# Decays relative to a tile's edge or the half's end: the reference column as the bias of ScalarE's exponential, tile by tile, instead of a subtraction on VectorE

## The chip, the cores and the metric

One core of one Trainium2 chip. The metric is the device time of one execution in microseconds (us); the profile is that of one execution, read on the same core.

## The reference

The program runs two transformer-like blocks over 256 tokens of width 2048. The part at issue is the RWKV-7 recurrence of the second block, 16 heads of 64:

```python
log_w = -jax.nn.softplus(-(w0 + jnp.tanh(pw) @ w2)) - 0.5
decay = jnp.exp(-jnp.exp(log_w))
...
def step(state, xs_t):
    r_t, w_t, k_t, v_t, kk_t, a_t = xs_t
    sa = jnp.einsum('bhvk,bhk->bhv', state, -kk_t)
    state = (state * w_t[:, :, None, :] + sa[..., None] * (kk_t * a_t)[:, :, None, :]
             + v_t[..., None] * k_t[:, :, None, :])
    return state, jnp.einsum('bhvk,bhk->bhv', state, r_t)
```

With s = sigmoid(w0 + ...), the logarithm of the decay is -exp(-0.5) s. The product of decays between two positions is therefore exp(-DECAY x (difference of two running sums of s)), with DECAY = exp(-0.5).

## The kernel before

The heads are taken in two halves of 8 (`hf` = 0, 1), one after the other, and the tokens in two tiles of 128, so the recurrence becomes matrix products inside a tile plus a state between the two tiles. In each half the operands lie as [128 partitions, J = 4, T = 256]: 1024 columns, j the pair of heads, two token tiles of 128 in each j. `CUM` is the running sum of s within each tile, `LDX` the same without the token's own share. R, K, KKN and AA are the receptance, the key, the normalised key and KKN times the gate a.

Each operand is multiplied by a decay relative to some reference point, so that the exponentials stay in range. There are four kinds of reference: the middle of each block of 64 tokens (`mid`, for KRD and BKD), the last token of the first half of each tile (`edge`, for KRO and BKO, which serve the block below the diagonal), the end of the first tile (`end`, for BKS, which carries the state), and the tile's start (nothing to subtract, for KRS).

VectorE (`rw_dve`, from L2079) forms the differences: `arg` (L2131) writes one into `EA[0]` or `EA[1]` and raises `decay_arg`. ScalarE (`rw_act`, from L1133) works through the list `tasks`: nine Exp instructions (L1166), each waiting for its `decay_arg` count and, through `decay_used`, until VectorE has done with the former contents of the buffer `EX[0]` or `EX[1]`. Behind the fourth and the fifth ScalarE also copies a tile of values out of PSUM (L1169). VectorE waits for Exp n with `expo(n)` and multiplies (`mul`, L2137). In order of VectorE's program between these: the bonus (L2157), the product BKO that raises `grams_ready`, an addition to the residual rows (`out_add`, L2087), BKS that raises `bks_ready`, and KRS that raises `decayed`.

The four differences for `edge` and `end` are of 512 columns, and so are the four Exps that read them. `EX[0]` and `EX[1]` are used several times, so the order of Exps and products is tied on both sides.

TensorE (`rw_pe`, from L2977) meanwhile multiplies pieces of the output projection (L2970). It then waits for `grams_ready`, takes the first pair of heads (L3036, L3044), waits for `bks_ready`, transposes BKS (L3029), which ScalarE copies out (L1172), and goes on with the other seven pairs, whose results VectorE masks (L2181). GpSimd clears a buffer after `decayed`. All engines run their own program in order; only semaphores tie them. No DMA is issued for this work.

Of the kernel before, what the change touches and what calls it, by code (L numbers as in the profile page):

```python
# [21 lines left out]
ALU = mybir.AluOpType  # L22
ACT = mybir.ActivationFunctionType
AX = mybir.AxisListType

P = 128
T = 256
# [18 lines left out]
DECAY = float(np.exp(-0.5))  # L46
# [85 lines left out]
def build(nc, a, out):  # L132
    ctx = ExitStack()
    with ctx:
# [47 lines left out]
        ev = Signals()  # L182
# [18 lines left out]
        def av(off, *dims):  # L201

            n = int(np.prod(dims))
            assert off + n <= 36984
            v = AR[:, off:off + n]
            if len(dims) == 2:
                v = v.rearrange("p (a b) -> p a b", a=dims[0])
            if len(dims) == 3:
                v = v.rearrange("p (a b c) -> p a b c", a=dims[0], b=dims[1])
            if len(dims) == 4:  # L210
                v = v.rearrange("p (a b c d) -> p a b c d", a=dims[0], b=dims[1], c=dims[2])
            return v
# [147 lines left out]
        J, HH = 4, 8  # L360
# [7 lines left out]
        EA = [YT[:, 12:16, :], av(21760, J, T)]  # L368
        EX = [av(33554, J, T), av(22784, J, T)]
# [8 lines left out]
        LDX = av(24576, J, T)  # L378
        AA = av(25600, J, T)
        CUM = av(34578, J, T)  # L380
# [4 lines left out]
        RY2 = av(35602, NT, 512)  # L385
        SAB = av(18432, 512)
        RST = av(36640, 4, 16)
        KSQ, RKP = av(0, J, T), av(5120, J, T)


# [20 lines left out]
        def part(x, n):  # L411

            return x[:, 2 * n:2 * n + 2, :].rearrange("p j (a s) -> p (j a) s", s=P)
# [3 lines left out]
        def flat(ap):  # L417
            n = len(ap.shape)
            if n == 3:
                return ap.rearrange("p a b -> p (a b)")  # L420
            if n == 4:
                return ap.rearrange("p a b c -> p (a b c)")
            return ap
# [709 lines left out]
        def rw_act(act, o, hf):  # L1133
            R, K, V = (RKVS[hf][:, w] for w in range(3))
            if hf == 1:
                act.wait_ge(ev["gn_out"], 2)
            for j in range(J):
                ins = nc.scalar.activation(KSQ[:, j, :], K[:, j, :], ACT.Square, scale=col2("kk", J * hf + j))
            o.tell(ins, ev["kk_sq"])
            for n, (dst, bias) in enumerate(((LDX, "w0"), (AA, "a0"), (GATE, None))):  # L1140
                act.wait_ge(ev["lora_mm"], 3 * hf + n + 1)
                for j in range(J):
                    b = 2 * (n % 2) + j // 2
                    src = PQ[:, b, (j % 2) * T:(j % 2 + 1) * T]
                    if bias:
                        ins = nc.scalar.activation(dst[:, j, :], src, ACT.Sigmoid, bias=col2(bias, J * hf + j))
                    else:
                        ins = nc.scalar.copy(dst[:, j, :], src)
                o.tell(ins, ev["lora_out"])
                if n == 1:  # L1150
                    act.wait_ge(ev["kk_mm"], hf + 1)
                    o.tell(nc.scalar.activation(KNORM[0:8, :], PP[0:8, 1, 0, 0:T], ACT.Sqrt), ev["kk_root"])
                    act.wait_ge(ev["lora_out"], 3 * hf + 2)
                    for j in range(J):
                        ins = nc.scalar.activation(EA[0][:, j, :], AA[:, j, :], ACT.Identity, scale=col2("ka", J * hf + j),
                                                   bias=OKA[:, J * hf + j:J * hf + j + 1])
                    o.tell(ins, ev["ka_out"])
            tasks = [(EX[0], EA[0], 1, 0, -1.0), (EX[1], EA[0], 1, 0, 1.0), (EX[0], EA[1], 2, 1, -1.0),
                     (part(EX[1], 0), part(EA[0], 0), 3, 2, -1.0), (part(EX[1], 1), part(EA[0], 1), 4, 2, -1.0),
                     (part(EX[0], 0), part(EA[1], 0), 5, 3, -1.0), (part(EX[0], 1), part(EA[1], 1), 6, 3, -1.0),  # L1160
                     (part(EX[1], 0), CUM[:, :, P:T], 6, 4, -1.0), (part(EX[1], 1), LDX[:, :, P:T], 6, 5, -1.0)]
            for n, (dst, src, args, uses, sign) in enumerate(tasks):
                act.wait_ge(ev["decay_arg"], 6 * hf + args)
                if uses:
                    act.wait_ge(ev["decay_used"], 5 * hf + uses)
                o.tell(nc.scalar.activation(dst, src, ACT.Exp, scale=sign * DECAY), ev["decay_exp"])  # L1166
                if n == 3 or n == 4:
                    act.wait_ge(ev["rv_turned"], 2 * hf + n - 2)
                    o.tell(nc.scalar.copy(VTK[:, n - 3, :], PQ[:, n - 3, :]), ev["rv_tok"])  # L1169
            for n in range(2):  # L1170
                act.wait_ge(ev["bk_turned"], 2 * hf + n + 1)
                o.tell(nc.scalar.copy(BKT[:, n, :], PQ[:, 2 + n, :]), ev["bk_tok"])  # L1172

            for m in range(16):
                act.wait_ge(ev["gram_diag"], 16 * hf + m + 1)
                o.tell(nc.scalar.copy(GR[0:64, m, :, 64:P], PP[0:64, (m % 4) // 2, m % 2, 0:256].rearrange("p (a t) -> p a t", a=4)),
                       ev["gram_out"])
            inverse_act(act, o, 1 + hf, GR[:, :, 0, :], RTI, RTT)
            for t in range(NT):
                n = 2 * hf + t + 1  # L1180
                act.wait_ge(ev["gn_mean"], n)
                o.tell(nc.scalar.activation(RY2[:, t, :], RY[:, t, :], ACT.Square), ev["gn_sq"])
                if t == 0:
                    nc.scalar.activation(SM[:, 8:9], EPSC, ACT.Sqrt)
                act.wait_ge(ev["gn_sum"], n)
                o.tell(nc.scalar.activation(RST[:, 1, 8 * t:8 * t + 8], RST[:, 0, 8 * t:8 * t + 8], ACT.Sqrt, scale=1.0 / 64,
                                            bias=RWEPSC), ev["gn_root"])
            if hf == 0:
                o.tell(nc.scalar.activation(RS, SS, ACT.Sqrt, scale=1.0 / D, bias=EPSC), ev["norm_root"])
# [889 lines left out]
        def rw_dve(dve, o, v, hf, diagonal):  # L2079
# [17 lines left out]
            for j in range(J):  # L2097
                for t in range(NT):
                    ins = v.tensor_tensor_scan(CUM[:, j, t * P:(t + 1) * P], ONES, LDX[:, j, t * P:(t + 1) * P], 0.0,
                                               ALU.mult, ALU.add)  # L2100
# [6 lines left out]
            for j in range(J):  # L2107
                ins = v.scalar_tensor_tensor(KKN[:, j, :], K[:, j, :], col2("kk", J * hf + j),
                                             PQ[:, 2 + j // 2, (j % 2) * T:(j % 2 + 1) * T], ALU.mult, ALU.mult)
# [3 lines left out]
            for j in range(J):  # L2113
                ins = v.scalar_tensor_tensor(RKP[:, j, :], R[:, j, :], col2("rk", J * hf + j), K[:, j, :], ALU.mult, ALU.mult)
# [2 lines left out]
            blocks = lambda x: x.rearrange("p j (b s) -> p (j b) s", s=64)  # L2117
            tiles = lambda x: x.rearrange("p j (t s) -> p (j t) s", s=P)
            mid = blocks(CUM)[:, :, 31:32].broadcast_to([P, 16, 64])
            edge = tiles(CUM)[:, :, 63:64].broadcast_to([P, 8, 64])  # L2120
            end = CUM[:, :, P - 1:P].broadcast_to([P, J, P])
            lo, hi = (lambda x: tiles(x)[:, :, 0:64]), (lambda x: tiles(x)[:, :, 64:P])

            half_of = lambda x, n: flat(x)[:, 512 * n:512 * (n + 1)]
            h = lambda x, n: half_of(x, n).rearrange("p (b s) -> p b s", s=64)
            w = lambda x, n: half_of(x, n).rearrange("p (j s) -> p j s", s=P)
            osl = lambda x: x.rearrange("p j t s -> p (j t) s")
            t0, t1 = (lambda x: x[:, :, 0:P]), (lambda x: x[:, :, P:T])

            def arg(out, x, y):  # L2130
                o.tell(v.tensor_tensor(out, x, y, ALU.subtract), ev["decay_arg"])  # L2131
# [4 lines left out]
            def mul(out, x, y):  # L2136
                return v.tensor_tensor(out, x, y, ALU.mult)  # L2137
# [3 lines left out]

            arg(blocks(EA[0]), blocks(CUM), mid)
            arg(blocks(EA[1]), blocks(LDX), mid)
            o.done(mul(AA, AA, KKN))
            expo(1)
            spent(mul(KRD[:, :, 1, :], R, EX[0]))
            expo(2)
            arg(h(EA[0], 0), hi(CUM), edge)
            arg(h(EA[0], 1), hi(LDX), edge)
            mul(BKD[:, 0], AA, EX[1])  # L2150
            spent(mul(BKD[:, 1], K, EX[1]))
            expo(3)
            arg(h(EA[1], 0), edge, lo(CUM))
            arg(w(EA[1], 1), end, t0(CUM))
            spent(mul(KRD[:, :, 0, :], KKN, EX[0]))
            dve.wait_ge(ev["bonus_mm"], hf + 1)
            o.tell(v.tensor_tensor(flat(BON), PQ[:, 2:4, :].rearrange("p a b -> p (a b)"), flat(V), ALU.mult), o.order)  # L2157
# [1 line left out]
            for j in range(J):  # L2159
                ins = mul(KRO[:, j, 1], h(EX[1], 0)[:, 2 * j:2 * j + 2, :], hi(R)[:, 2 * j:2 * j + 2, :])  # L2160
            spent(ins)
            expo(5)
            for j in range(J):
                ins = mul(KRO[:, j, 0], h(EX[1], 1)[:, 2 * j:2 * j + 2, :], hi(KKN)[:, 2 * j:2 * j + 2, :])
# [24 lines left out]
            n = 2 * hf  # L2189
# [53 lines left out]
            for j in range(J):  # L2243
                ins = v.scalar_tensor_tensor(BON[:, j, :], BON[:, j, :], col2("lnb", J * hf + j), GATE[:, j, :], ALU.add, ALU.mult)
# [1152 lines left out]
```

## Time and profile before

| | us |
|---|---|
| median of 3 runs | 3686.59 |
| lowest and highest | 3685.14, 3688.18 |
| the profiled execution | 3684.46 |
| its span in the profile | 3682.7 |

| engine | busy us | share of the span |
|---|---|---|
| TensorE (PE) | 3531.0 | 96% |
| TensorE weight loads (PEld) | 3084.2 | 84% |
| VectorE (DVE) | 2328.9 | 63% |
| ScalarE (ACT) | 1476.9 | 40% |
| GpSimd (POOL) | 77.2 | 2% |

The names in brackets are those of the profile's rows. Shares are over the whole span and hide that the stages differ; the stretch of the change is under 19 us long and comes twice. A matmul's end is modelled, and a few records can be missing. The idle time that a row shows is that of its engine just before it, with the instruction that ended it. Tiles of the large working buffer all have the name `arena`, columns of constants `constants`, PSUM banks `quad` and `pairs`.

### The profile page before, as it was taken

To read this page: it belongs to the slowest core of one execution; us is meant where nothing else is said; L and a number is where in the kernel's file an instruction comes from. 1 tells how busy PE (TensorE), PEld (TensorE's weight loads), DVE (VectorE), ACT (ScalarE), POOL (GpSimd) and SP (SyncE) were. 2 spreads that over 40 slices of the span, in tenths; PEclk is the share of its full clock that TensorE was granted. 3 is DMA by queue.
4 is the path that set the end of the run, shared out by engine and by line. 5 is a ranking of instruction groups with operands and counts; after the bars stand their busy time and mean duration, and the time that the engine had idled before them with its cause. 6 is when DMAs were issued, how large, how long until landed. Compare 5 with 4: busy or idle time off the path is not lost.

```text
span 3682.7 us, 51878 instructions
## 1 busy us (share of the span) xinstructions
PE 3531.0 (96%) x21246; PEld 3084.2 (84%) x21246; DVE 2328.9 (63%) x2679; ACT 1476.9 (40%) x1313; POOL 77.2 (2%) x110
## 2 busy tenths in 40 slices
PE   8997899999999999999999999988989989999998
PEld 8985799999988888888888799986657778888887
DVE  3655547977767776666666766466674556666666
ACT  4333433345543333333333433443332433333333
POOL 1000000000000000000000000000100000000000
PEclk9998999999999999999999999999999999999999
DMA  5552444556677675555555455431114445555553
GB/s 195 183 183 71 169 157 175 203 185 222 223 265 243 242 255 202 203 197 205 203 201 204 150 181 176 161 114 46 47 69 149 149 149 191 186 193 184 192 188 143
DMA packets 122755, 649.47 MB, mean 176 GB/s; under 512 B 10720, under 2 KB 43872, under 8 KB 49536
## 3 DMA queue, kind: packets, MB, share of 16 engines
q1 hardware_dynamic: 116368, 621.25, 47.7%
q0 software_dynamic: 6256, 26.34, 1.9%
q8 instruction: 98, 1.61, 0.2%
q14 instruction: 33, 0.27, 0.0%
HBM read 619.76 MB, written 27.79 MB: 176 GB/s over the span
## 4 chain that ended last, share of the span: by engine, by line
PE 89%; DVE 8%; ACT 2%; issue 1%; DMA 0%; ACTq 0%; DVEq 0%; SPq 0%; PEldq 0%
PE pairs L2569 20%; PE pairs L2570 20%; PE pairs L2571 20%; PE quad L2614 13%; PE quad L2615 6%; DVE w_low L2280 2%; PE quad L2655 2%; PE pairs L2970 1%; PE quad L3161 1%; PE pairs L2742 1%; DVE arena L2137 1%; ACT w_high L1209 0%; PE quad L2722 0%; PE quad L3036 0%; DVE arena L1738 0%
## 5 line engine op out<-in xcount | busy, mean ns | idle before, releaser
L2280 DVE TENSOR_TENSOR w_low<-ring,w_high 128x2048 fp32r<-128x2048 f32 (+1 forms) x540 | 1233.1, 2284 | 879.8 <-ACT w_high L1209 879.4
L1209 ACT CAST w_high<-ring 128x2048 fp32r<-128x2048 f32 (+1 forms) x540 | 1026.3, 1901 | 1681.5 <-PE pairs L2571 1220.0
L2569 PE MATMUL pairs<-x_t,w_high 128*128 128x256 f32 x2608 | 744.1, 285 | 8.1 <-DVE w_low L2280 7.6
L2570 PE MATMUL pairs<-x_t,w_high 128*128 128x256 f32 x2608 | 738.5, 283 | 0.0
L2571 PE MATMUL pairs<-x_t,w_low 128*128 128x256 f32 x2608 | 738.4, 283 | 0.0
L2614 PE MATMUL quad<-x_t,w_high 128*128 128x512 f32 x1984 | 703.7, 399 | 9.9 <-DVE w_low L2280 9.9
L2569 PE MATMUL pairs<-w_high,act_high 128*128 128x512 f32 x1568 | 611.6, 390 | 5.4 <-ACT arena L759 3.5
L2570 PE MATMUL pairs<-w_low,act_high 128*128 128x512 f32 x1568 | 610.9, 390 | 0.0
L2571 PE MATMUL pairs<-w_high,act_low 128*128 128x512 f32 x1568 | 610.7, 389 | 0.0
L2615 PE MATMUL quad<-x_t,w_low 128*128 128x256 f32 x1984 | 557.7, 281 | 0.0
L2569 PEld LDWEIGHTS pairs<-x_t,w_high 128*128 128x128 f32 x2608 | 499.5, 192 | 13.0 <-issue 8.6
L2570 PEld LDWEIGHTS pairs<-x_t,w_high 128*128 128x128 f32 x2608 | 499.7, 192 | 0.7 <-issue 0.2
L2571 PEld LDWEIGHTS pairs<-x_t,w_low 128*128 128x128 f32 x2608 | 499.4, 192 | 0.3
L2614 PEld LDWEIGHTS quad<-x_t,w_high 128*128 128x128 f32 x1984 | 373.6, 188 | 102.7 <-DVE w_low L2280 10.2
L2615 PEld LDWEIGHTS quad<-x_t,w_low 128*128 128x128 f32 x1984 | 375.6, 189 | 1.1
L2569 PEld LDWEIGHTS pairs<-w_high,act_high 128*128 128x128 f32 x1568 | 294.6, 188 | 69.0 <-issue 5.9
L2571 PEld LDWEIGHTS pairs<-w_high,act_low 128*128 128x128 f32 x1568 | 294.7, 188 | 61.7
L2570 PEld LDWEIGHTS pairs<-w_low,act_high 128*128 128x128 f32 x1568 | 294.7, 188 | 59.9
L1500 DVE TENSOR_TENSOR x_res<-x_res,pairs 128x1024 f32<-128x1024 f32 x128 | 156.1, 1220 | 78.9 <-PE pairs L2571 78.0
L2569 PE MATMUL pairs<-w_high,x_t 128*128 128x512 f32 x384 | 151.5, 395 | 9.5 <-DVE w_low L2280 9.5
L2570 PE MATMUL pairs<-w_low,x_t 128*128 128x512 f32 x384 | 150.5, 392 | 0.0
L2571 PE MATMUL pairs<-w_high,x_t 128*128 128x512 f32 x384 | 150.4, 392 | 0.0
(542 smaller groups left out, 2897.4 us busy)
## 6 DMA issues: line engine op xcount, KB each, us to landing
ring<-pu SPq DMA_DIRECT2D x128, 1024.0 KB, 4.8
ring<-pv SPq DMA_DIRECT2D x128, 1024.0 KB, 4.8
ring<-f SPq DMA_DIRECT2D x128, 1024.0 KB, 4.7
ring<-win SPq DMA_DIRECT2D x48, 1024.0 KB, 4.8
ring<-dn SPq DMA_DIRECT2D x32, 1024.0 KB, 4.7
ring<-rw SPq DMA_DIRECT2D x24, 1024.0 KB, 4.8
ring<-wout SPq DMA_DIRECT2D x16, 1024.0 KB, 4.7
ring<-wq SPq DMA_DIRECT2D x16, 1024.0 KB, 4.8
```

Of the source, the lines that this page charges most:

```text
L1209: nc.scalar.copy(WH[s % 2][:, 0:w], flat(ring[s])[:, 0:w]).then_inc(ev["split_high"], 1)
L1500: v.tensor_tensor(X[:, :, cols], X[:, :, cols], PP[:, (UNIT0["peer"] + nb) % 2], ALU.add).then_inc(ev["dve_free"], 1)
L2137: return v.tensor_tensor(out, x, y, ALU.mult)
L2280: v.tensor_tensor(WL[s % 2][:, 0:w], flat(ring[s])[:, 0:w], WH[s % 2][:, 0:w].bitcast(F32), ALU.subtract).then_inc(ev["split_low"], 1)
L2569: mm(out, stat[0], mov[0], start=start, stop=False, skip_group_check=True)
L2570: mm(out, stat[0], mov[1], start=False, stop=False, skip_group_check=True)
L2571: return mm(out, stat[1], mov[0], start=False, stop=stop, skip_group_check=True)
L2614: mm(PQ[:, m, :], wh[:, k, cols], XTB[:, :, kt, :], start=(kt == 0), stop=False, skip_group_check=True)
L2615: ins = mm(PQ[:, m, 0:T], wl[:, k, cols], XTH[:, kt, :], start=False, stop=(kt == KT - 1), skip_group_check=True)
L2655: ins = mm(PQ[:, 2 + b, t * P:(t + 1) * P], A0[:, b, t, :], B0[:, b, t, :], start=True, stop=True)
L2742: ins = mm(PP[:, q % 2, 0, m * P:(m + 1) * P], M1B[:, q % 2, m, :], Tt[:, 4 * q + m, :], start=True, stop=True)
L2970: ins = mm(o_bank(q)[:, t], YT[:, kt0 + k, t * P:(t + 1) * P], OW[o_buffer(q)][:, k, :], start=opens and k == 0, stop=closes and k == 3, s ...
```

## The change

Four of the six differences of each half are no longer formed. In their place VectorE writes 20 columns `EDGE`: DECAY times CUM at each tile's edge (8 columns), the same negated (8), and minus DECAY times CUM at the first tile's end (4). ScalarE adds such a column as the bias of the Exp. A bias is one value per partition, and the reference differs from tile to tile, so one Exp can cover only one tile's part: 64 columns for an edge, 128 for the end. Task by task ScalarE now issues 1, 1, 1, 8, 8, 8, 4, 1, 1 Exps instead of nine single ones. The waits for `decay_used`, the two copies and the order of the products are kept; `decay_arg` is raised 3 times in each half instead of 6, the third time by the last of the EDGE columns.

```diff
+        EDGE = av(36704, 20)
...
-            tasks = [(EX[0], EA[0], 1, 0, -1.0), (EX[1], EA[0], 1, 0, 1.0), (EX[0], EA[1], 2, 1, -1.0),
-                     (part(EX[1], 0), part(EA[0], 0), 3, 2, -1.0), (part(EX[1], 1), part(EA[0], 1), 4, 2, -1.0),
-                     (part(EX[0], 0), part(EA[1], 0), 5, 3, -1.0), (part(EX[0], 1), part(EA[1], 1), 6, 3, -1.0),
-                     (part(EX[1], 0), CUM[:, :, P:T], 6, 4, -1.0), (part(EX[1], 1), LDX[:, :, P:T], 6, 5, -1.0)]
-            for n, (dst, src, args, uses, sign) in enumerate(tasks):
-                act.wait_ge(ev["decay_arg"], 6 * hf + args)
+            eighth = lambda x, n: flat(x)[:, 64 * n:64 * (n + 1)]
+
+            def whole(dst, src, sign):
+                return nc.scalar.activation(dst, src, ACT.Exp, scale=sign * DECAY)
+
+            def behind_edge(first, src):
+                for i in range(8):
+                    ins = nc.scalar.activation(eighth(EX[1], first + i), src[:, i // 2, P * (i % 2) + 64:P * (i % 2) + P], ACT.Exp,
+                                               scale=-DECAY, bias=EDGE[:, i:i + 1])
+                return ins
+
+            def ahead_of_edge():
+                for i in range(8):
+                    ins = nc.scalar.activation(eighth(EX[0], i), CUM[:, i // 2, P * (i % 2):P * (i % 2) + 64], ACT.Exp,
+                                               scale=DECAY, bias=EDGE[:, 8 + i:9 + i])
+                return ins
+
+            def ahead_of_end():
+                for j in range(J):
+                    ins = nc.scalar.activation(flat(EX[0])[:, 512 + P * j:512 + P * (j + 1)], CUM[:, j, 0:P], ACT.Exp,
+                                               scale=DECAY, bias=EDGE[:, 16 + j:17 + j])
+                return ins
+
+            tasks = [(lambda: whole(EX[0], EA[0], -1.0), 1, 0), (lambda: whole(EX[1], EA[0], 1.0), 1, 0),
+                     (lambda: whole(EX[0], EA[1], -1.0), 2, 1), (lambda: behind_edge(0, CUM), 3, 2),
+                     (lambda: behind_edge(8, LDX), 3, 2), (ahead_of_edge, 3, 3), (ahead_of_end, 3, 3),
+                     (lambda: whole(part(EX[1], 0), CUM[:, :, P:T], -1.0), 3, 4),
+                     (lambda: whole(part(EX[1], 1), LDX[:, :, P:T], -1.0), 3, 5)]
+            for n, (task, args, uses) in enumerate(tasks):
+                act.wait_ge(ev["decay_arg"], 3 * hf + args)
                 if uses:
                     act.wait_ge(ev["decay_used"], 5 * hf + uses)
-                o.tell(nc.scalar.activation(dst, src, ACT.Exp, scale=sign * DECAY), ev["decay_exp"])
+                o.tell(task(), ev["decay_exp"])
...
+            v.tensor_scalar(EDGE[:, 0:8], tiles(CUM)[:, :, 63:64].rearrange("p a o -> p (a o)"), DECAY, None, ALU.mult)
+            v.tensor_scalar(EDGE[:, 8:16], tiles(CUM)[:, :, 63:64].rearrange("p a o -> p (a o)"), -DECAY, None, ALU.mult)
+            o.tell(v.tensor_scalar(EDGE[:, 16:20], CUM[:, :, P - 1:P].rearrange("p a o -> p (a o)"), -DECAY, None, ALU.mult),
+                   ev["decay_arg"])
             o.done(mul(AA, AA, KKN))
...
-            arg(h(EA[0], 0), hi(CUM), edge)
-            arg(h(EA[0], 1), hi(LDX), edge)
             mul(BKD[:, 0], AA, EX[1])
             spent(mul(BKD[:, 1], K, EX[1]))
             expo(3)
-            arg(h(EA[1], 0), edge, lo(CUM))
-            arg(w(EA[1], 1), end, t0(CUM))
             spent(mul(KRD[:, :, 0, :], KKN, EX[0]))
```

## Rows read from the trace of the kernel before

**Rows 1.** The page: the chain that ended last, by engine, whole kernel
```profile
PE 89%; DVE 8%; ACT 2%; issue 1%; DMA 0%; ACTq 0%; DVEq 0%; SPq 0%; PEldq 0%
```

**Rows 2.** Stretches, one per half: length; busy PE, PEld, DVE, ACT, POOL; clock, DMA
```profile
2552.24:2571.03 18.79, 14.58 (x58) 7.38 (x56) 18.72 (x29) 8.66 (x13) 0.61 (x1) 1.00 0.32 113
2678.63:2697.43 18.80, 14.59 (x59) 7.39 (x57) 18.73 (x29) 8.66 (x13) 0.61 (x1) 1.00 0.31 112
```

**Rows 3.** The chain that ended last, first half: start, us, what
```profile
2552.24 2.36 DVE arena L2131 x2
2554.60 1.14 DVE arena L2137
...
2555.76 1.23 DVE arena L2137
2556.99 1.20 DVE arena L2131 x2
2558.20 2.27 DVE arena L2137 x2
2560.47 1.21 DVE arena L2131 x2
2561.67 1.13 DVE arena L2137
2562.80 1.14 DVE arena L2157
2563.94 2.82 DVE arena L2137 x10
2566.76 1.20 DVE x_res L2087 x2
2567.95 1.22 DVE arena L2137 x2
...
2569.21 0.67 PE quad L3029 x4
...
2569.91 1.08 ACT arena L1172 x2
```

**Rows 4.** TensorE in order of time, with idle time before and its releaser
```profile
2566.90 1.13 PE L3036 MATMUL quad<-arena 64*128 64x256 f32 x8 [2.93 <-DVE arena L2137]
```

**Rows 5.** ScalarE in order of time, first half: start, us, instruction
```profile
2560.56 0.63 ACT L1166 ACTIVATE arena<-arena 128x512 f32<-128x512 f32 x1 [2.42 <-DVE arena L2137]
2561.10 0.57 ACT L1169 COPY arena<-quad 128x512 f32<-128x512 f32 x1
2561.56 0.63 ACT L1166 ACTIVATE arena<-arena 128x512 f32<-128x512 f32 x1
```

**Rows 6.** ScalarE's groups by line and shape: busy us, mean ns of one
```profile
L1166 ACT ACTIVATE arena<-arena 128x512 f32<-128x512 f32 x12 | 7.3, 628 | 7.2 <-DVE arena L2137 7.2
...
L1166 ACT ACTIVATE arena<-arena 128x1024 f32<-128x1024 f32 x6 | 6.1, 1053 | 15.7 <-DVE arena L2131 12.5 <-DVE arena L2137 3.2
...
L1138 ACT ACTIVATE arena<-arena,constants 128x256 f32<-128x256 f32 x8 | 3.4, 496 | 1.2 <-DVE arena L2225 1.2
...
L951 ACT ACTIVATE arena<-arena 128x256 f32<-128x256 f32 x1 | 0.4, 402 | 0.0
```

**Rows 7.** ScalarE in order of time: the four Squares of the keys
```profile
2532.87 1.69 ACT L1138 ACTIVATE arena<-arena,constants 128x256 f32<-128x256 f32 x4
```

**Rows 8.** VectorE's groups by line and shape: busy us, mean ns of one
```profile
L2213 DVE TENSOR_SCALAR arena<-arena 128x8 f32<-128x8 f32 x4 | 0.7, 172 | 0.1
```

**Rows 9.** TensorE after two longer idle times elsewhere, and stretches with clock
```profile
775.37 1.16 PE L2655 MATMUL quad<-arena 128*128 128x128 f32 x8 [3.54 <-DVE arena L1547]
...
1046.02 0.49 PE L2569 MATMUL pairs<-w_high,act_high 128*128 128x512 f32 x1 [3.50 <-ACT arena L759]
...
1046.00:1049.00 3.00, 2.98 (x8) 2.38 (x9) 2.18 (x5) 0.00 (x0) 0.80 (x2) 0.61 1.03 400
775.00:778.00 3.00, 2.16 (x12) 1.98 (x13) 3.00 (x7) 1.06 (x1) 0.00 (x0) 0.83 0.00 0
```

More of the change, by code:

```diff
@@ L2119, in rw_dve @@
             mid = blocks(CUM)[:, :, 31:32].broadcast_to([P, 16, 64])
-            edge = tiles(CUM)[:, :, 63:64].broadcast_to([P, 8, 64])
-            end = CUM[:, :, P - 1:P].broadcast_to([P, J, P])
             lo, hi = (lambda x: tiles(x)[:, :, 0:64]), (lambda x: tiles(x)[:, :, 64:P])
```

## The prediction

> **What bounds the kernel now.** I read the chain that ended last first, for the whole kernel: TensorE carries 89% of it and VectorE 8% [rows 1]. The change touches none of the large TensorE loops; it sits in two short stretches, one per half of the RWKV heads, where the decayed operands are made. So the second view is the table of stretches, from the first difference to the first product that needs all results. The two stretches are alike to 0.01 us: 18.79 and 18.80 us, VectorE busy for 18.72 and 18.73 of them, ScalarE for 8.66, TensorE for 14.6 at clock 1.00, which is the 2.4 GHz level [rows 2]. VectorE is full and ScalarE half empty. The third view is the chain inside the first stretch: it runs on VectorE from 2552.24 to 2569.17 without a break, over the four differences that the change takes away (two at 2556.99, two at 2560.47), and only then passes to TensorE, ScalarE and TensorE [rows 3]. TensorE's own rows say the same from the other side: it stands idle 2.93 us until 2566.90, released by VectorE [rows 4]. What VectorE saves here shortens the kernel; what ScalarE makes VectorE wait lengthens it. I work out one half and double it, since each half is serial with the next and the rows repeat.
>
> **What is removed.** Four 512-column differences leave VectorE: 1.20 us for one pair and 1.21 for the other [rows 3], 2.41 us per half, all on the chain.
>
> **What is added to VectorE.** Three tiny multiplications (8, 8 and 4 columns) make EDGE, ahead of the multiplication of AA. A multiplication of 128x8 takes 0.17 us alone [rows 8]. Without a wait between them neighbours overlap, so three cost between 0.24 (about half of each hidden, my assumption) and 0.52 (none hidden); I take 0.30. Were ScalarE never late, the half would gain 2.41 - 0.30 = 2.1 us, the kernel 4.2 us. That is the ceiling of any gain: 0.11%.
>
> **What ScalarE gets.** Four Exp instructions of 512 columns (the ones that read the differences) become 28: eight of 64 columns three times, four of 128 once, each with a bias column. No row shows a 64-column Exp, so I bound it by neighbours. Exp takes 0.628 us for 512 columns and 1.053 for 1024, so 0.83 ns a column [rows 6]. An activation that reads one per-partition column as operand (the Square of the keys, its scale) takes 0.496 us at 256 columns; one without such a column takes 0.402 [rows 6]. Hence 64 columns with a bias: 0.496 - 192 x 0.00083 = 0.337 us; 128 columns: 0.390. Four of those Squares in a row take 1.69 us [rows 7], so they start (1.69 - 0.496)/3 = 0.398 us apart: neighbours overlap by 0.098. The spacing is then 0.239 us at 64 columns and 0.292 at 128. Eight of 64 end 7 x 0.239 + 0.337 = 2.01 us after they start and let the next start after 1.91, where one 512-column Exp ended after 0.63 and let the next start after 0.54 [rows 5]. Bounds: 0.145 (the row without a column, less the same overlap) and 0.337 (no overlap). I take 0.239, whose row is nearest in kind.
>
> The Trainium skill (ScalarE: Activation LUTs, What ACT_TABLE_LOAD costs) prices an activation with a pointer bias at 280 + 0.833 N ns and the overlap at 93 ns; its spacing at 64 columns would be 240 ns, an estimate from that page, and its sum the one below. The Trainium skill (VectorE: DVE Perf Modes, The TRN2 errata) speaks against the change: a fixed latency is paid per instruction that reads SBUF, and it asks for tiles of at least 512 elements. The rows agree in that 64 columns come to 0.337 us by them, against 0.628 for 512.
>
> **The schedule, first half.** VectorE ends the second difference at 2554.60, EDGE at 2554.90; AA (1.16 with its wait) to 2556.06; the product that uses the first Exp (1.23) to 2557.29; the two BKD products (2.27) to 2559.56 [durations of rows 3]. That frees EX[1]. It was freed at 2560.47, and Exp started at 2560.56 [rows 3, 5]; now ScalarE starts at 2559.65. The first eight end at 2561.66. The copy of the values starts at 2561.56 and, as now, holds the next back by 0.46 [rows 5]; the second eight run 2562.02 to 2564.03; the second copy takes 0.46; the third eight (for the end of a tile's first half) run 2564.39 to 2566.40; the four of 128 follow to 2567.57. The two last whole Exps end near 2568.6, before they are wanted.
> VectorE meanwhile: KRD 1.13 to 2560.69, bonus 1.14 to 2561.83. The group of ten at 2563.94 [rows 3] is eight products of 128 columns and two of 512; the two are 1.20, so each four small ones take 0.81. The first four run to 2562.64 unhindered. The second four must wait for 2564.03 and end at 2564.89. The two BKO products must wait for 2566.40 and run 2566.45 to 2567.65, which answers to 2566.76 before. Then the addition to x_res (1.20) and the two BKS products (1.22) to 2570.07, against 2569.17 before [rows 3]. So 0.90 us later per half: of the 2.1 us gained, 3.0 are handed back in two waits for ScalarE (about 1.4 and 1.6 us). Behind the waiting VectorE instruction stand all its later ones, and TensorE waits for them: its idle time grows from 2.93 to 3.83 us. Its first pair of products (1.7 us) ends before 2570.07, so it adds nothing. The next stages (transposes, ScalarE's two copies, the pairs) have the same lengths and start 0.90 us later; ScalarE is free for its copies by then. GpSimd's memset that waits for the same end feeds a much later stage.
>
> Sum: 2 x 0.90 = +1.8 us. The profiled execution took 3684.46 us (span 3682.70 and 1.76 around it), 2.13 below the median of 3686.59; carried to the median, 3686.59 + 1.8 = 3688.4 us. The runs before lie within 3 us of each other; 0.2% (7.4 us, so 3679.2 and 3694.0) is about what a measurement of this kernel can tell from no change.
>
> **Rivals.**
> *ScalarE's short instructions are cheap enough.* Break-even: BKO must start by 2565.56 as before, so ScalarE has 2565.56 - 0.05 - 0.10 - 2559.65 = 5.76 us, less 0.92 of copies, for 24 instructions: a spacing of 0.20 us. At the lower bound of 0.145 BKO starts at 2564.20, a gain of 1.36 us per half: 3686.59 - 2.7 = 3683.9. For it: only a 256-column row gives the cost of the operand column. Against it: that row has the operand column as these do. With no delay at all, 3682.4.
> *The short instructions do not overlap* (a spacing of 0.337): 24 x 0.098 = 2.35 us more per half, together 2 x 3.25 = +6.5, 3693.1. Against it: the four Squares overlap and write one tile too.
> *TensorE's clock falls in the longer idle time: the way to slower.* In both halves the clock stayed at 1.00 after 2.93 us of idling [rows 2, 4]. After idle times of 3.54 and 3.50 us elsewhere it fell to the 1.2 GHz level near the restart: it is 0.83 in the 3 us at 775 and 0.61 in the 3 us at 1046 [rows 9]. The idle time would now be 3.83. If the clock falls at the restart, the first pair (1.7 us) doubles, of which about 0.5 is slack before the BKS products end, then the transposes (0.67) double: about 1.2 us per half, 3686.59 + 2 x (0.90 + 1.2) = 3690.8. It decides for slower by over 0.2% from 3.7 us per half, so 2.8 from the clock: it would have to stay low over the next pairs too, each of some 1.65 us. Against it: at 1046 the row's 0.61 comes to (1 - 0.61)/0.5 x 3 = 2.3 us at the low level, which covers the first pair and the transposes and not much more [rows 9]. The Trainium skill (TensorE: Matmul & The Clock Gate, Why this matters for your kernels) asks for no TensorE gaps over about 3 us; by that rule the idle time steps over the line in both halves and the time would be about 3690.8, and the two rows after 3.5 us of idling agree.
> *Another cover.* If the differences had not been on the chain, nothing would change; the unbroken chain speaks against it.
>
> **How the numbers follow.** Forecast (ScalarE becomes the bound, clock unmoved): 0.52, 3686.5 to 3690. Short instructions cheap: 0.17, 3682.4 to 3686. Clock falls: 0.21, 3689.5 to 3694, of it 0.04 beyond. No overlap: 0.08, about 3693. Anything else: 0.02. All but the far end of the clock case, a part of the no-overlap case with the scatter of runs, and the unknown lie within 0.2%: same 0.93, slower 0.06, faster 0.01. The range takes the forecast, most of the cheap case and most of the clock case: 3684.0 to 3692.6.
>
> **What would show it.** In the changed profile: 28 Exps per half with bias, spaced 0.24 us; four differences fewer, three multiplications of 4 or 8 columns; VectorE idle some 1.4 us before the second four small products and 1.6 before BKO, both put down to ScalarE; TensorE's idle time 3.8 us; the BKS products ending 0.9 us later against the first difference. Wrong if the spacing is nearer 0.15 (VectorE hardly waits and TensorE's idle time shrinks to about 1.6 us), if EDGE costs far from 0.3, or if the clock after the restart reads below 1.00.

## The result, and the profile after

The change makes the kernel a little slower: the ratio of its time to that before is 1.0015, 95% interval 1.0009 to 1.0021, which is 5.5 us on 3686.6. The medians of 20 runs each are 3693.16 us (3690.07 to 3696.41) and 3686.73 (3684.26 to 3692.99). The profiled execution has a span of 3689.5 us against 3682.7. The forecast was 3688.4 with a range to 3692.6. The ratio, applied to the 3686.59 of the forecast, puts the time at 3692.1, near the range's upper end; the median of 3693.16 by itself lies 0.6 above it. The shift is under 0.2%, as forecast, but three times the size that the sum gave, and the time falls among those that the forecast gave to its rival, the fall of the clock (3689.5 to 3694).

The chain of the changed kernel in the first half (start, us, what) answers to [rows 3]:

```profile
2552.25 2.36 DVE arena L2154 x2
...
2554.62 0.14 DVE arena L2168
2554.77 0.07 DVE arena L2169
2554.84 1.14 DVE arena L2160
...
2556.00 3.51 DVE arena L2160 x3
...
2559.59 1.58 ACT arena L1166 x7
...
2561.61 0.47 ACT arena L1194
2562.08 1.25 ACT arena L1166 x6
...
2564.00 0.47 ACT arena L1194
...
2565.09 1.30 ACT arena L1172 x5
...
2566.42 1.29 DVE arena L2160 x2
2567.72 1.19 DVE x_res L2112 x2
2568.91 1.22 DVE arena L2160 x2
...
2570.17 1.98 PE quad L3052 x8
...
2572.17 0.59 ACT arena L1197
...
2572.81 1.13 PE quad L3059 x8
```

The chain was on VectorE without a break; now it leaves VectorE when the BKD products end and runs through ScalarE's short Exps and both copies until 2566.40. The BKS products end at 2570.12, where it was 2569.17. Then come the eight transposes (L3052) in 1.98 us, and ScalarE's second copy waits for the last of them. In the kernel before, the first four took 0.67 us and the second four were hidden behind the first copy [rows 3].

ScalarE and VectorE in order of time, the same stretch (start, us, instruction, idle time before it):

```profile
2559.59 2.02 ACT L1166 ACTIVATE arena<-arena 128x64 f32<-128x64 f32 x8 [1.21 <-DVE arena L2160]
2561.52 0.56 ACT L1194 COPY arena<-quad 128x512 f32<-128x512 f32 x1
2561.98 2.02 ACT L1166 ACTIVATE arena<-arena 128x64 f32<-128x64 f32 x8
...
2564.37 2.02 ACT L1172 ACTIVATE arena<-arena 128x64 f32<-128x64 f32 x8
2566.29 1.27 ACT L1178 ACTIVATE arena<-arena 128x128 f32<-128x128 f32 x4
```

```profile
2554.53 0.16 DVE L2167 TENSOR_SCALAR arena<-arena 128x8 f32<-128x8 f32 x1
...
2561.69 0.88 DVE L2160 TENSOR_TENSOR arena<-arena 128x128 f32<-128x128 f32 x4
2564.03 0.90 DVE L2160 TENSOR_TENSOR arena<-arena 128x128 f32<-128x128 f32 x4 [1.47 <-ACT arena L1166]
2566.42 1.29 DVE L2160 TENSOR_TENSOR arena<-arena 128x512 f32<-128x512 f32 x2 [1.49 <-ACT arena L1172]
```

VectorE waits 1.47 us for the second eight Exps and 1.49 for the third. The groups by line and shape give the price of one:

```profile
L1166 ACT ACTIVATE arena<-arena 128x64 f32<-128x64 f32 x32 | 8.1, 336 | 2.4 <-DVE arena L2160 2.4
...
L1178 ACT ACTIVATE arena<-arena 128x128 f32<-128x128 f32 x8 | 2.5, 396 | 0.0
```

TensorE's rows, first half and then second:

```profile
2567.86 1.13 PE L3059 MATMUL quad<-arena 64*128 64x256 f32 x8 [3.88 <-DVE arena L2160]
2568.96 1.12 PE L3067 MATMUL pairs<-arena 64*64 64x128 f32 x8
2570.17 1.97 PE L3052 MATMUL quad<-constants,arena 128*128 128x128 f32 x8
2572.81 1.13 PE L3059 MATMUL quad<-arena 64*128 64x256 f32 x8 [0.68 <-ACT arena L1197]
```

```profile
2697.28 2.08 PE L3059 MATMUL quad<-arena 64*128 64x256 f32 x8 [5.01 <-DVE arena L2160]
2699.29 1.12 PE L3067 MATMUL pairs<-arena 64*64 64x128 f32 x8
2700.34 1.94 PE L3052 MATMUL quad<-constants,arena 128*128 128x128 f32 x8
```

The idle time before the pairs is 3.88 us in the first half and 5.01 in the second, against 2.93 [rows 4]. The second is longer because TensorE's own pieces there ended 10.60 us after the first difference (2697.28 - 5.01 - 2681.67), 1.1 us sooner than before. The reason lies just ahead of the first difference of the second half. The kernel before ran its pieces at half the clock there (first line, clock in the third column from the end), the changed kernel did not (second line):

```profile
2674.90:2677.90 3.00, 3.00 (x5) 1.13 (x4) 2.93 (x6) 0.00 (x0) 0.00 (x0) 0.50 0.00 0
2677.90:2680.90 3.00, 3.00 (x9) 1.23 (x7) 2.93 (x6) 0.00 (x0) 0.00 (x0) 1.00 0.00 0
```

So TensorE's work gets done sooner and it waits longer for the same VectorE. In e3, e7 and v2 (below), whose clock was up there too, the second idle time is likewise 1.13 us longer than the first; in e4, where it was not, both are 1.65. The eight products that took 1.13 take 2.08 in the second half, and the transposes 1.97 and 1.94. The table of stretches says why (length; busy PE, PEld, DVE, ACT, POOL; then the granted clock, the DMA share and GB/s):

```profile
2569.00:2572.00 3.00, 2.91 (x16) 2.25 (x16) 2.97 (x5) 0.59 (x1) 0.62 (x1) 0.50 0.02 5
2606.50:2609.50 3.00, 3.00 (x17) 3.00 (x16) 0.27 (x2) 0.00 (x0) 0.00 (x0) 0.51 0.00 0
2696.00:2699.00 3.00, 1.72 (x8) 1.28 (x8) 3.00 (x6) 2.02 (x6) 0.00 (x0) 0.50 0.12 49
```

The clock is at its lower level, 0.50 or 1.2 GHz, in all three (0.51 where the window takes in a little of the higher level). In the kernel before it is 1.00 at the first two times:

```profile
2569.00:2572.00 3.00, 2.06 (x16) 1.54 (x16) 2.75 (x5) 1.59 (x4) 1.58 (x1) 1.00 0.00 0
2606.50:2609.50 3.00, 3.00 (x29) 3.00 (x29) 1.60 (x3) 0.59 (x1) 1.28 (x1) 1.00 0.00 0
```

To say how much each part took I cut the second block's recurrence at marks that every profile has: the first difference of a half (A0, A1), the first transpose of BKS (S0, S1), the first product of the second pair (P0, P1) and the first transposed rows of the memory (E). From P to the next mark lie the other pairs, the triangular inverse and the recurrence itself. All in us, from the starts of those instructions:

| kernel | A0 to S0 | S0 to P0 | P0 to A1 | A1 to S1 | S1 to P1 | P1 to E | A0 to E |
|---|---|---|---|---|---|---|---|
| before | 16.97 | 1.82 | 107.60 | 16.98 | 1.82 | 99.85 | 245.04 |
| before, another execution | 16.98 | 1.82 | 107.59 | 16.98 | 1.81 | 99.89 | 245.07 |
| changed | 17.92 | 2.64 | 108.86 | 18.67 | 2.62 | 101.20 | 251.91 |
| changed, another execution | 17.92 | 2.65 | 108.86 | 18.66 | 2.61 | 101.21 | 251.91 |
| e1, changed, 7 idle-time products | 20.13 | 1.82 | 107.24 | 20.13 | 1.82 | 98.40 | 249.54 |
| e2, before, 6 idle-time products | 18.47 | 1.82 | 109.23 | 18.46 | 1.82 | 100.04 | 249.84 |
| e3, before, 0.9 us of delay | 17.88 | 2.65 | 108.74 | 18.62 | 2.65 | 101.38 | 251.92 |
| e4, changed, no bias column | 15.70 | 1.82 | 108.89 | 15.70 | 1.81 | 101.27 | 245.19 |
| e5, changed, 3 idle-time products | 17.92 | 1.82 | 108.86 | 17.92 | 1.82 | 99.86 | 248.20 |
| e6, before, 3 idle-time products | 16.97 | 1.82 | 107.58 | 16.97 | 1.82 | 99.87 | 245.03 |
| e7, before, 0.4 us of delay | 17.38 | 2.64 | 108.88 | 18.13 | 2.64 | 100.06 | 249.73 |
| v2, bias ahead of the edge and end only | 16.28 | 1.82 | 107.60 | 17.02 | 1.96 | 98.41 | 243.09 |
| v2 with 2 idle-time products | 16.26 | 1.82 | 107.62 | 16.27 | 1.82 | 101.31 | 245.10 |

The marks repeat within 0.05 us from one execution of a kernel to another, although A0 itself came at 2552.24 in one execution of the kernel before and at 2554.62 in the other. So a difference of 0.5 us inside these stretches is real where one between two whole times is not. From A0 to E the change costs 251.91 - 245.04 = 6.87 us.

### The profile page after: what moved, and what is told of

Read it like the earlier page. It is cut to its first block, busy times and chain, and to the rows that moved or that the text cites. A ratio compares the mean times of both kernels' runs of the same rounds, so it can differ in the third digit from the quotient of the medians.

```text
span 3689.5 us, 51924 instructions
## 1 busy us (share of the span) xinstructions
PE 3534.4 (96%) x21246; PEld 3088.5 (84%) x21246; DVE 2324.3 (63%) x2677; ACT 1485.6 (40%) x1361; POOL 77.0 (2%) x110
## 4 chain that ended last, share of the span: by engine, by line
PE 89%; DVE 8%; ACT 2%; issue 1%; DMA 0%; ACTq 0%; DVEq 0%; SPq 0%; PEldq 0%
PE pairs L2592 20%; PE pairs L2593 20%; PE pairs L2594 20%; PE quad L2637 13%; PE quad L2638 6%; DVE w_low L2303 2%; PE quad L2678 2%; PE pairs L2993 1%; PE quad L3184 1%; PE pairs L2765 1%; PE quad L3059 0%; ACT w_high L1234 0%; PE quad L2745 0%; DVE arena L2160 0%; PE quad L2760 0%
```

## The experiments

**e1: keep TensorE busy in the changed kernel.** Theory 1 was that two things add up, ScalarE's delay and the fall of TensorE's clock in the longer idle time; theory 2, that the schedule alone explains the time. Products that nobody reads fill the idle time.

```diff
             pe.wait_ge(ev["rv_tok"], 2 * hf + 2)
+            for _ in range(7):
+                mm(PQ[:, 0, :], ONES, flat(M4), start=True, stop=True)
             pe.wait_ge(ev["grams_ready"], hf + 1)
```

> The changed kernel with seven idle-time products (128x512, results never read) on TensorE before it waits for the BKO products, in each half. Theory 1 (ScalarE's delay plus TensorE's clock): the low-clock stretches that begin near 2569 and 2696 us vanish, the second pair starts about 0.8 us earlier in the first half and 1.5 us earlier in the second; the delay by ScalarE (0.95 us per half) stays; in all 2 to 4 us less than the changed kernel, so 1.5 to 4 us above the kernel before. Theory 2 (only the schedule, the clock a bystander): the time is that of the changed kernel, ratio to before 1.0015.

Ratio to before 1.0016 (1.0007 to 1.0025). The dose was wrong. TensorE in order of time:

```profile
2564.18 6.28 PE L3046 MATMUL quad<-constants 128*128 128x512 f32 x14 [0.54 <-ACT arena L1194]
2570.39 1.14 PE L3061 MATMUL quad<-arena 64*128 64x256 f32 x8
```

Seven such products are 14 instructions and take 6.28 us, so the pairs start at 2570.39, late by the fillers themselves: 20.13 us to S0 instead of 17.92. But the clock stayed up: 1.82 us from S to P in both halves, and the long stretches are the shortest of all, 107.24 and 98.40. The fillers cost 2.21 us in the first half and 1.46 in the second (20.13 against 18.67), and from A0 to E that was more than regained (249.54 against 251.91). The whole-kernel ratio shows no such gain. It puts the time 5.9 us above before, beyond theory 1's 1.5 to 4 and close to theory 2's 1.0015, but the overrun of the fillers, which neither theory had, is in it. So the run speaks for the mechanism by its rows alone: the clock did not fall.

**e2: the control.** The same lines in the kernel before, with `range(6)`.

> The control: the kernel before with six such products in the same place. Its clock was at the high level there already. Both theories: the same time within 1 us, unless keeping TensorE busy moves a later fall of the clock (then up to 2 us either way).

Ratio 1.0016 (1.0007 to 1.0025); the expectation missed. Six were too many as well: 18.47 us to S0 instead of 16.97, both halves, and the stretch P0 to A1 grew to 109.23. The control shows the overrun. It also shows a later stretch growing behind an overrun, where those of e1 shrank behind one.

**e3: the delay without ScalarE.** One useless multiplication on VectorE, in the kernel before, ahead of BKO.

```diff
             expo(5)
...
+            v.tensor_tensor(flat(EA[0])[:, 0:800], flat(AA)[:, 0:800], flat(K)[:, 0:800], ALU.mult)
             expo(6)
             mul(osl(BKO[:, 0]), lo(AA), h(EX[0], 0))
```

> The kernel before with one VectorE multiplication of 800 columns (0.9 us, its result is overwritten unread) ahead of the BKO products, in each half; ScalarE's work is untouched. Theory 1: the same two clock falls as in the changed kernel come although ScalarE does nothing new, and the time is 4 to 7 us above before. Theory 2: 2 x 0.9 = 1.8 us above before, ratio 1.0005.

Ratio 1.0023 (1.0013 to 1.0032). The stretches have the lengths of the changed kernel: 17.88, 2.65, 108.74, 18.62, 2.65, 101.38, in all 251.92 against 251.91. TensorE:

```profile
2571.18 1.13 PE L3037 MATMUL quad<-arena 64*128 64x256 f32 x8 [3.83 <-DVE arena L2137]
...
2573.49 1.97 PE L3030 MATMUL quad<-constants,arena 128*128 128x128 f32 x8 [0.29 <-DVE arena L2137]
2576.14 2.08 PE L3037 MATMUL quad<-arena 64*128 64x256 f32 x8 [0.68 <-ACT arena L1172]
```

After 3.83 us of idling the transposes take 1.97 us and the first eight products of the second pair 2.08. Theory 2 expected +1.8 us and is refuted: 0.9 us of work on VectorE costs 6.9, as the change does, though ScalarE does nothing new. That the two sums agree to 0.01 us is luck in one stretch, P0 to A1. In the changed kernel the second pair ran at the full clock (1.13 us) and the clock fell again in the inverse, near 2606.5. In e3 the first fall lasts on over the pairs (first line), and at the inverse, just as far behind P0, the clock is up (second line):

```profile
2576.20:2579.20 3.00, 3.00 (x18) 1.84 (x18) 0.00 (x0) 0.42 (x2) 0.31 (x1) 0.50 0.00 0
2610.10:2613.10 3.00, 2.29 (x20) 2.29 (x21) 1.49 (x3) 1.09 (x3) 0.50 (x1) 1.00 0.00 0
```

**e4: the bias column.** The 28 short Exps without `bias`, all with `scale=-DECAY`. This leaves out the reference points of the decays; the instructions and sizes stay.

```diff
-                                               scale=DECAY, bias=EDGE[:, 8 + i:9 + i])
+                                               scale=-DECAY)
```

> The changed kernel with the 28 short Exps without bias column and all with the negative scale: this leaves out the reference points, so the decays are not the right ones; instructions and sizes stay. If the bias column is what costs: spacing 0.145 us instead of 0.24 at 64 columns, VectorE's waits shrink from 1.47 and 1.49 us to under 1 in sum, the BKO products start about 1.3 us earlier than in the kernel before, the time is 2 to 5 us below before (the clock stays high). If the short length is what costs whatever the operands: spacing stays above 0.2 and the time within 2 us of before or above.

Ratio 1.0001 (0.9992 to 1.0010). ScalarE's group and VectorE's wait:

```profile
L1166 ACT ACTIVATE arena<-arena 128x64 f32<-128x64 f32 x32 | 5.1, 242 | 2.4 <-DVE arena L2160 2.4
```

```profile
2567.03 1.76 DVE L2160 TENSOR_TENSOR arena<-arena 128x128 f32<-128x128 f32 x8
2569.54 1.29 DVE L2160 TENSOR_TENSOR arena<-arena 128x512 f32<-128x512 f32 x2 [0.75 <-ACT arena L1172]
```

One Exp takes 0.242 us instead of 0.336; eight in a row take 1.28 instead of 2.02, a spacing of (1.28 - 0.242)/7 = 0.148. Of the two waits one is gone and the other is 0.75 us. Up to S the half gains 1.27 us on before, as expected, and 2.2 on the changed kernel: without the column as operand the short Exps are quick enough to beat the subtractions; with it they are not. The whole is not faster, though: P0 to A1 is 108.89 and P1 to E 101.27, so of the 2.55 us that the two stretches gain against before the next ones take 2.71 back. The expected gain of 2 to 5 us was wrong by that.

**e5 and e6: idle-time products of the right length.** `range(3)`, in the changed kernel and in the kernel before.

> The changed kernel with three idle-time products on TensorE per half instead of seven. The first trial showed that each is two instructions of 0.44 us, so seven took 6.2 us and held the pairs back themselves; three take 2.6 us and end before the BKO products do. Theory 1 (clock): first difference to transposes 17.9 us in both halves (changed kernel 17.92 and 18.67), transposes to second pair 1.82 us in both (2.64 and 2.62), so 2.4 us less than the changed kernel over the two stretches; 1.9 us above the kernel before there. Theory 2 (schedule only): 17.92 and 18.67, 2.64 and 2.62 stay.

> The control with three such products in the kernel before: 16.97 and 1.82 us in both halves, as without them. If the fillers by themselves cost something, the first exceeds 17.1. Total within 2 us of before; a later fall of the clock may move.

e5: ratio 1.0009 (0.9999 to 1.0018); e6: 1.0003 (0.9994 to 1.0012). TensorE in the second half of e5:

```profile
2693.83 2.84 PE L3046 MATMUL quad<-constants 128*128 128x512 f32 x6 [1.67 <-ACT arena L1194]
2697.08 1.13 PE L3061 MATMUL quad<-arena 64*128 64x256 f32 x8 [0.40 <-DVE arena L2160]
...
2699.48 1.09 PE L3054 MATMUL quad<-constants,arena 128*128 128x128 f32 x8 [0.55 <-DVE arena L2160]
2701.30 1.13 PE L3061 MATMUL quad<-arena 64*128 64x256 f32 x8 [0.73 <-ACT arena L1197]
```

The six instructions of 0.44 us end 0.40 us before the pairs may start; the eight products take 1.13 again and the transposes 1.09. S0 - A0 is 17.92 in both halves and P - S 1.82 in both, exactly as theory 1 had it, and the control stands at 16.97 and 1.82. What is left between e5 and e6 in these stretches is the schedule alone: 0.95 us per half. But P0 to A1 is 108.86 in e5, as in the changed kernel, and 107.58 in e6: keeping the clock up in the short stretch did not bring that part back.

**v2: a part of the change.** VectorE subtracts for the decays behind the edge as before; the bias serves those ahead of the edge and of the end, 12 short Exps instead of 28.

```diff
             expo(2)
+            arg(h(EA[0], 0), hi(CUM), edge)
+            arg(h(EA[0], 1), hi(LDX), edge)
             mul(BKD[:, 0], AA, EX[1])
```

> Part of the change alone: the bias for the decays ahead of the edge and of the end (12 short Exps), VectorE subtracts again for those behind the edge. By the spacings read (0.24 and 0.29 us) ScalarE ends the eight at about the time VectorE wants them: first difference to transposes 16.2 us, 0.8 less than before, VectorE's wait at most 0.3. If the number of short Exps is not what costs, it is near 17.9 as in the full change. Total: 1.6 us below before if the clock falls stay as they were; up to 1.5 above if they move.

> The same with two idle-time products (1.75 us) per half. First difference to transposes 16.2 us as without them; if TensorE's clock is what decides the rest, the total is the lowest of all: 2 to 5 us below before. If not, as v2_ahead_only.

Ratios 0.9998 (0.9989 to 1.0007) and, with two idle-time products, 0.9999 (0.9990 to 1.0008): the same as before. VectorE waits 0.27 us for the eight Exps:

```profile
2565.26 1.70 DVE L2155 TENSOR_TENSOR arena<-arena 128x128 f32<-128x128 f32 x8
2567.22 1.29 DVE L2155 TENSOR_TENSOR arena<-arena 128x512 f32<-128x512 f32 x2 [0.27 <-ACT arena L1166]
```

A0 to S0 is 16.28 us, 0.69 less than before, where 0.8 was expected. In the second half of v2 the clock fell all the same, after 3.36 us of idling, which ate the gain (17.02 and 1.96); with idle-time products it did not (16.27 and 1.82). But there P1 to E is 101.31 instead of 99.85, so that the whole gains nothing. The lowest A0 to E of all is v2's 243.09, by a P1 to E of 98.41 without a fall of the clock in it. Most of this 1.95 us is gone by the end of the program: from E on the profiled execution of v2 takes 887.1 us, those of the kernel before 885.5 and 885.7. Neither version is shown to beat the kernel before.

**e7: less delay.** As e3 with 320 columns.

> The kernel before with a VectorE multiplication of 320 columns (about 0.4 us) ahead of the BKO products instead of 800. TensorE's idle time becomes 3.3 us, between 2.93 (clock kept) and 3.83 (clock lost). If the clock falls above some idle time near 3 us: transposes to second pair 2.6 us as with the 0.9 us delay. If the fall needs more: 17.4 and 1.82 us in both halves.

```profile
2568.01 1.14 PE L3037 MATMUL quad<-arena 64*128 64x256 f32 x8 [3.33 <-DVE arena L2137]
...
2570.32 1.97 PE L3030 MATMUL quad<-constants,arena 128*128 128x128 f32 x8 [0.53 <-DVE arena L2137]
2572.96 2.08 PE L3037 MATMUL quad<-arena 64*128 64x256 f32 x8 [0.68 <-ACT arena L1172]
```

One execution, 3691.12 us (3684.85 for the kernel before beside it). Here an idle time of 3.33 us was followed by the fall: 2.64 us from S to P in both halves. 0.41 us of delay costs 249.73 - 245.04 = 4.69 us.

**The two kernels again.**

> The changed kernel, another execution: do the stretches repeat? If the clock falls in the two stretches belong to the kernel: transposes to second pair 2.6 us in both halves again, and the inverse stages (107.6 and 99.9 us before, 108.9 and 101.2 in the first profile) within 0.3 of the first profile. If they are chance: between the values of before and after.

> The kernel before, another execution: 16.97 and 1.82 us in both halves; inverse stages 107.6 and 99.9 us if their clock falls belong to the kernel, anything from 107.2 to 108.9 and from 98.4 to 101.3 (the values seen so far over all kernels) if they are chance.

3691.96 and 3687.11 us, one execution each. Every stretch came back within 0.05 us. The falls of the clock that lengthen the stretches came again in both: they belong to the kernel, not to chance. One that lengthens nothing did not: in the kernel before, the clock was 0.50 from 2712.50 to 2715.50, at the pieces of the output projection, and at the same work of the second execution (2714.90 to 2717.90) it was 1.00, with P1 to E at 99.85 and 99.89.

## Why the prediction was right about the scale and short in size

The range held because it took in most of the rival case. The case to which the forecast gave 0.52, a delay by ScalarE with the clock unmoved, did not come; the one to which it gave 0.21 did. That the number was in range is owed to the width of the range, not to the sum.

*What bounds the stretch*: right. The chain ran on VectorE, and 0.9 us put on it alone (e3) shifted all that follows.

*What VectorE saves*: right. The three EDGE instructions took 0.23 us on the chain (2554.61 to 2554.84), where 0.30 was taken.

*What ScalarE gets*: right to a hundredth. A 64-column Exp with bias took 0.336 us (0.337 by the sum), eight in a row 2.02 (2.01), one of 128 columns 0.396 (0.390). The Trainium skill (ScalarE: Activation LUTs, What ACT_TABLE_LOAD costs) gives about 93 ns for each operand that is read from such a column. The traces agree: 0.336 with it less 0.242 without it (e4) is 0.094 us.

*The schedule*: right. ScalarE started at 2559.59 (2559.65 in the sum), VectorE waited 1.47 and 1.49 us (1.4 and 1.6), the BKS products ended 0.95 us later than before (0.90). With the clock kept (e5) the two stretches cost 1.9 us, the forecast's 1.8.

*The clock unmoved*: this step failed. The prediction took the clock as staying at 1.00 and gave its fall 0.21. The fall came in both halves, as the rival had it: in the first it began near 2569, after the first eight products of the pair, in the second some two microseconds before the restart. The longer idle time did it: e3 had the falls without ScalarE's work, e5 had ScalarE's work without the falls. At this place the clock stayed up after 1.65, 2.23 and 2.93 us of idling (e4, the first half of v2, and the kernel before in both halves of both executions), and was lost at 3.33, 3.36, 3.83, 3.88, 4.46, 4.96 and 5.01 us. The Trainium skill (TensorE: Matmul & The Clock Gate, Why this matters for your kernels) asks for no gap over about 3 us. At this place the traces agree; elsewhere they show falls beside shorter gaps, 1.97 us before the inverse of the changed kernel, so a gap below 3 us is no safeguard.

*The price of the clock*: the rival's 1.2 us per half does not follow from its own terms. A pair of 1.7 us that doubles, less 0.5 of slack, and transposes of 0.67 that double make 1.9. Measured are 0.82 in the first half (2.64 - 1.82), where the fall spared the first eight products, and 0.75 + 0.80 in the second: 2.37 in all. That this is 1.2 on average is luck. The rival's reason against a higher price was mis-sized too: it read 2.3 us of low clock at 1046 from a window that ends before the clock recovers. The windows 1045 to 1048 (clock 0.78) and 1048 to 1051 (0.66) together make (0.22 + 0.34)/0.5 x 3 = 3.4.

*The later stretches*: the remaining 6.87 - 1.90 - 2.37 = 2.60 us were in no part of the sum: P0 to A1 grew by 1.26 and P1 to E by 1.35. The sum carried these stretches over at their old length; that was the second omission. The kernels measured show what they cost. From 2604.21 to 2612, in the inverse, the chain of the kernel before runs on TensorE alone; in the changed kernel the clock is low from about 2606.5 for some three microseconds there. In P1 to E there are two such places, about 34 and 60 us behind P1.

The 13 profiles sort by the number of falls at these places or over the first pairs. The table gives, in whole us behind P0 or P1, where the granted clock goes to 0.50; a star marks those places, and "on" a low clock that lasts on from the stretch before for over 3 us of the pairs.

| kernel | falls after P0 | P0 to A1 | falls after P1 | P1 to E |
|---|---|---|---|---|
| e1 | none | 107.24 | none | 98.40 |
| v2 | none | 107.60 | none | 98.41 |
| before, another execution | 104 | 107.59 | 59* | 99.89 |
| before | 104 | 107.60 | 15, 59* | 99.85 |
| e6 | 15, 104 | 107.58 | 15, 59* | 99.87 |
| v2 with 2 idle-time products | none | 107.62 | 34*, 61* | 101.31 |
| e5 | 14, 35* | 108.86 | 60* | 99.86 |
| e2 | 14, 34*, 106 | 109.23 | 14, 34* | 100.04 |
| e7 | on* | 108.88 | on* | 100.06 |
| e3 | on* | 108.74 | 34*, 61* | 101.38 |
| e4 | 34*, 105 | 108.89 | 33*, 61* | 101.27 |
| changed, both executions | 34* | 108.86 | 33*, 61* | 101.20 |

P0 to A1 takes 107.2 to 107.6 us with no star and 108.7 to 109.2 with one; P1 to E takes 98.4 with none, 99.9 to 100.1 with one and 101.2 to 101.4 with two. So one such fall comes with some 1.3 or 1.4 us, and the changed kernel has one more than before in each of the two stretches. The falls without a star, beside pieces of the output projection, cost nothing that the marks show.

*Not settled*: what decides whether a fall comes at these places. e4, whose halves have no long idle time and end earlier, has them as the changed kernel does; e5, whose long idle times are filled, has that of the first half; e6 has those of before; e1 has none. So the shift of the work decides in some way, but no run changed it by itself. The share of ScalarE's delay and of the first falls is shown by experiments; that of the later falls is read from the clock in all profiles, and no experiment isolated it.

## What to carry to other kernels

Cutting one long instruction on an idle engine into short ones to relieve a full engine pays only while the short ones end before they are wanted: here 24 of them at 0.24 us did not fit into a place for 24 at 0.20, and 12 of them did, but for a wait of 0.27 us. Price each at its fixed part plus the operand column, and lay out both engines in time before counting the saving. Then look at what the bound engine's lateness does to TensorE: a wait that grows from 2.9 to 3.3 us can cost more through the clock than the wait itself, and idle-time products that end before the wait does take that price away at the place itself, though not in the stages behind it; count their instructions first.

## What the runs showed of the hardware that was not expected

A delay of 0.41 us in each half cost 4.69 us from A0 to E, and one of 0.9 us cost 6.88. A float32 product of 512 columns is two instructions of 0.44 us on TensorE (14 instructions for seven, 6.28 us). The stretches of a kernel repeat to 0.05 us while the time at which they begin differs by 2.4 us between two executions of the same program. A kernel whose work in two stretches became 2.55 us shorter (e4) was no faster, since the clock then fell in later stages, at the inverse of both halves. Such a fall comes with some 1.3 or 1.4 us where the chain runs on TensorE and with nothing beside pieces that nobody waits for yet.
